# 32 conditioning blocks of a diffusion trunk, multiplied by VectorE during the first input projection

## What is computed

```
ada = silu(cond) @ w_ada[i] + b_ada[i]          # cond: c_ctx and c; 6 x 1024 outputs per layer, 2 layers
sh_m, sc_m, gt_m, sh_f, sc_f, gt_f = split(ada, 6)
h = x * (1 + sc_m) + sh_m
m = ssd_mixer(h) if i == 0 else gdn_mixer(h)    # h @ w_in -> conv -> scan -> norm -> @ w_out
x = layer_norm(ALPHA * x + gt_m * m)
x = layer_norm(ALPHA * x + gt_f * conv_glu_ffn(x * (1 + sc_f) + sh_f))
```

## Time and profile before

| | us |
|---|---|
| median of 3 runs | 1602.67 (1597.7 to 1603.6) |
| profiled execution, whole | 1600.62 |
| its span, first to last instruction | 1598.7 |
| TensorE busy | 1528.4 (96%) |
| VectorE / ScalarE / GpSimd busy | 872.5 / 799.5 / 905.3 |
| input projection, blocks 4 to 48 | about 45.6 to 238.2 |
| scan | about 238.2 to 401.1 |
| DMA queue q1 | 205.96 MB |

### The profile page before, as it was taken

One profiled execution on the slowest core, in us unless ns is written; L12 is line 12 of the kernel. 1 busy time (PEld: TensorE's weight loads), 2 busy tenths in 40 slices (PEclk: granted clock), 3 DMA queues, 4 the chain that ended last, 5 costly groups with the idle time before them and its releaser, 6 DMA issues.

```text
span 1598.7 us, 30956 instructions
## 1 busy us (share of the span) xinstructions
PE 1528.4 (96%) x11737; PEld 1452.6 (91%) x11737; DVE 872.5 (55%) x1814; ACT 799.5 (50%) x1461; POOL 905.3 (57%) x516
## 2 busy tenths in 40 slices
PE   8999999999999999999899999999889999999996
PEld 6999997887989999999899989778778989999996
DVE  3443105776447777613663449598873357777323
ACT  3655436776336544424766563656554345444332
POOL 2555556676563555657146556787763725555552
PEclk9999999999999999999999999999979999999998
DMA  9443437887351443434125323102123423444431
GB/s 376 122 124 114 131 121 269 307 297 279 122 151 56 129 130 120 147 123 152 53 80 173 96 92 104 41 28 54 41 81 119 148 77 106 131 120 139 140 114 40
DMA packets 58018, 209.65 MB, mean 131 GB/s; under 512 B 6320, under 2 KB 6448, under 8 KB 57648
## 3 DMA queue, kind: packets, MB, share of 16 engines
q1 hardware_dynamic: 56752, 205.96, 39.4%
q10 hardware_dynamic: 1152, 2.10, 0.4%
HBM read 200.63 MB, written 7.41 MB: 130 GB/s over the span
## 4 chain that ended last, share of the span: by engine, by line
PE 70%; issue 10%; DVE 9%; POOL 6%; ACT 4%; DMA 2%; POOLq 0%; SPq 0%; DVEq 0%; ACTq 0%
PE ps L900 6%; PE ps L902 6%; PE ps L901 6%; PE ps L808 6%; PE ps L810 6%; PE ps L809 6%; POOL wlo L332 4%; PE ps L1144 3%; PE ps L2884 3%; PE ps L1145 3%; PE ps L1146 3%; PE ps L2885 3%; PE ps L2886 3%; PE ps L402 2%; DVE ps L2457 2%
## 5 line engine op out<-in xcount | busy, mean ns | idle before, releaser
L332 POOL TENSOR_TENSOR wlo<-raw,whi 128x1024 fp32r<-128x1024 f32 (+1 forms) x191 | 484.3, 2536 | 416.0 <-ACT whi L320 415.7
L320 ACT ACTIVATE whi<-raw 128x1024 fp32r<-128x1024 f32 (+1 forms) x237 | 261.4, 1103 | 501.0 <-PE ps L810 186.9
L900 PE MATMUL ps<-hhi,whi 128*128 128x384 f32 x656 | 219.8, 335 | 2.5 <-POOL wlo L332 2.0
L974 DVE SCALAR_TENSOR_TENSOR evac<-ps,vec,evac 128x189 f32<-128x189 f32 (+3 forms) x440 | 166.5, 412 | 99.4 <-ACT evac L915 69.7
L902 PE MATMUL ps<-hhi,wlo 128*128 128x384 f32 x656 | 219.2, 334 | 0.0
L901 PE MATMUL ps<-hlo,whi 128*128 128x384 f32 x656 | 219.1, 334 | 0.0
L2649 POOL TENSOR_TENSOR wlo<-raw,whi 128x1024 fp32r<-128x1024 f32 x46 | 111.2, 2417 | 124.9 <-ACT whi L320 124.9
L2884 PE MATMUL ps<-hhi,whi 128*128 128x384 f32 x368 | 126.3, 343 | 1.7 <-POOL wlo L2649 1.7
L900 PEld LDWEIGHTS ps<-hhi,whi 128*128 128x128 f32 x656 | 123.1, 188 | 4.4 <-issue 3.2
L868 DVE SCALAR_TENSOR_TENSOR xr<-ps,ada,xr 128x128 f32<-128x128 f32 x64 | 23.8, 413 | 183.3 <-PE ps L810 183.2
L2886 PE MATMUL ps<-hhi,wlo 128*128 128x384 f32 x368 | 123.4, 335 | 0.0
(11 more groups left out here) (375 smaller groups left out, 3574.2 us busy)
## 6 DMA issues: line engine op xcount, KB each, us to landing
raw<-w_in_in SPq DMA_DIRECT2D x98, 512.0 KB, 3.6
raw<-w_up_in SPq DMA_DIRECT2D x88, 512.0 KB, 3.5
raw<-w_ada_in SPq DMA_DIRECT2D x80, 512.0 KB, 4.4
raw<-w_down_in SPq DMA_DIRECT2D x32, 704.0 KB, 4.0
raw<-w_out_in SPq DMA_DIRECT2D x32, 512.0 KB, 3.6
first_ada<-w_ada_in SPq DMA_DIRECT2D x16, 512.0 KB, 10.1
qe<-e_keep SPq DMA_DIRECT2D x8, 512.0 KB, 6.7
s<-s_ssd_in SPq DMA_DIRECT2D x8, 256.0 KB, 4.0
```

Source lines behind the costliest of these rows:

```text
L320: act.activation(whi[:, z.mod(SPL), 0:p.kt * P], raw[:, b.mod(RAW), 0:p.kt * P], ACT.Copy).then_inc(hi_ready, 1)
L332: pool.tensor_tensor(wlo[:, z.mod(SPL), 0:p.kt * P], raw[:, b.mod(RAW), 0:p.kt * P], whi[:, z.mod(SPL), 0:p.kt * P].bitcast(F32), ALU.subt ...
L900: pe.matmul(out, a, hhi[:, k, :], start=(k == 0), stop=False)
```

## The change

32 of the 80 later conditioning tiles (eight units of four) are no longer multiplied by TensorE in the scan. Their weights are loaded four blocks at a time (2 MB, two buffers) during the input projection. For each of the two rows of cond, VectorE multiplies the raw weights by silu(cond) as a per-partition scalar and sums over the eight tiles of the model width: 16 instructions of 128x512 per unit, accumulated in PSUM banks 6 and 7, the last of each row writing to SBUF. TensorE then sums the partitions with eight small matmuls per unit (`mid_fold`), after blocks 20, 23, 28, 33, 37, 40, 43 and 46; ScalarE copies the rows one step later, TensorE turns them into columns another step later, VectorE adds the bias. VectorE's products are spread over steps 9 to 32, two or three per step behind the taps; the remaining 59 follow without steps. SyncE issues the first two unit loads ahead of the load of block 8, after a wait for the first four blocks, and the others ahead of the loads of blocks 20, 26, 31, 36, 40 and 43, each after a wait for the products that free its buffer. `ADA_G` becomes 8, 6, 6, 6, 6, 6, 5, 5; the slots in `ssd_pe` are unchanged. The dt chain is moved three steps earlier and its sums to banks 5 and 4.

```diff
+MID = 8
+MID_B = 4
+MID_OPS = 2 * DT
+ADA_M = MID * MID_B
+ADA_2 = 2 * ADA_T - ADA_1 - ADA_M
...
+        MID_AT = (20, 23, 28, 33, 37, 40, 43, 46)
+        MID_LOAD = {20: 2, 26: 3, 31: 4, 36: 5, 40: 6, 43: 7}
+        MID_BIAS = {MID_AT[b] + 2: b for b in range(3)}
+        MID_STEP = {s: 2 if s < 12 else 3 for s in range(9, CONV_T + 1)}
+        MID_BANK, SUM_BANK = 4, 6
+
+        def mid_load(sp, b):
+            if b < 2:
+                sp.wait_ge(blk_done, SPL + FIRST)
+            else:
+                sp.wait_ge(ada_acc, MID_OPS * (b - 1))
+            j = ADA_1 + MID_B * b
+            sp.dma_start(mid_raw[:, b % 2, :, :], io["w_ada"][j:j + MID_B].rearrange("b p n -> p b n")).then_inc(first_in[b % 2], 16)
...
+        def mid_product(dve, m):
+
+            b, t, c = m // MID_OPS, m % MID_OPS // 2, m % 2
+            w = mid_raw[:, b % 2, :, t * P:(t + 1) * P]
+            run = ps[:, SUM_BANK + c, :].rearrange("p (b n) -> p b n", b=MID_B)
+            one = scond[:, t, ZW + c:ZW + c + 1]
+            if t == 0 and c == 0:
+                dve.wait_ge(first_in[b % 2], 64 + 16 * (b // 2 + 1))
+            if m > 1:
+                dve.wait_ge(ada_acc, m - 1)
+            if t == 0:
+                i = dve.tensor_scalar(run, w, one, None, ALU.mult)
+            elif t < DT - 1:
+                i = dve.scalar_tensor_tensor(run, w, one, run, ALU.mult, ALU.add)
+            else:
+                if b and c == 0:
+                    dve.wait_ge(ada_used, ADA_1 + b)
+                i = dve.scalar_tensor_tensor(mid_sum[:, c, :, :], w, one, run, ALU.mult, ALU.add)
+            i.then_inc(ada_acc, 1)
...
+        def mid_fold(pe, b):
+
+            pe.wait_ge(ada_acc, MID_OPS * (b + 1))
+            pe.wait_ge(ada_ready, 1 + DT + b)
+            pe.wait_ge(dt_dec, 1)
+            for n in range(2 * MID_B):
+                q = 32 * (n % 4)
+                mm = pe.matmul(ps[q:q + 32, MID_BANK, 0:P], mid_pick[:, 31 - n:63 - n], mid_sum[:, n % 2, n // 2, :],
+                               tile_position=(0, q), start=(n < 4), stop=(n >= 4))
+            mm.then_inc(ada_used, 1)
+
+        def mid_columns(pe, b):
+            pe.wait_ge(ada_row, DT + b + 1)
+            ada_columns(pe, MID_B, MID_BANK)
...
+                for _ in range(MID_STEP[s] if s in MID_STEP else 0):
+                    mid_product(dve, m)
+                    m += 1
+                if s in MID_BIAS:
+                    mid_bias(dve, MID_BIAS[s])
+            for m in range(m, MID * MID_OPS):
+                if m > 5 * MID_OPS and m % MID_OPS == DT:
+                    mid_bias(dve, m // MID_OPS - 2)
+                mid_product(dve, m)
+            for b in range(MID - 2, MID):
+                mid_bias(dve, b)
...
                 block(s, t % 4)
-                if s == 17:
+                if s == 14:
                     rate_rows()
-                if s == 19:
+                if s == 16:
                     rate_sums()
+                if s in MID_AT:
+                    mid_fold(pe, MID_AT.index(s))
+                if s - 2 in MID_AT:
+                    mid_columns(pe, MID_AT.index(s - 2))
...
-        ADA_G = (0, 14, 24, 34, 44, 53, 62, 71, ADA_2)
+        ADA_G = (0, 8, 14, 20, 26, 32, 38, 43, ADA_2)
...
-            steps(sp, FIRST + RAW, N_IN, lambda j: load_block(sp, sin, j))
+            mid_load(sp, 0)
+            mid_load(sp, 1)
+            for s in range(FIRST + RAW, N_IN):
+                if s in MID_LOAD:
+                    mid_load(sp, MID_LOAD[s])
+                load_block(sp, sin, Idx(s))
```

More of the change, by code:

```diff
@@ L219, in trunk @@
             if name == "ada_first":
-                own_n[kind] += n
+                own_n[kind] += n + MID
                 continue
@@ L270, in trunk @@
         ln_std, ln_stat = sem("ln_std"), sem("ln_stat")
-        x_kept, tri_ready = (sem(x) for x in ("x_kept", "tri_ready"))
+        x_kept, ada_acc = (sem(x) for x in ("x_kept", "ada_acc"))
         def raw_free(sp, at):
@@ new lines, in mid_bias @@
+        def mid_bias(dve, b):
+            dve.wait_ge(ada_tr, DT + b + 1)
+            ada_bias(dve, MID_BANK, ADA_1 + MID_B * b, MID_B).then_inc(ada_ready, 1)
+        def mid_fold(pe, b):
[7 more added lines that the diff above has]
+            mm.then_inc(ada_used, 1)
@@ L597, in h_ready, with mid_rows @@
+        def mid_columns(pe, b):
+            pe.wait_ge(ada_row, DT + b + 1)
+            ada_columns(pe, MID_B, MID_BANK)
+        def mid_rows(act, b):
+            act.wait_ge(ada_used, ADA_1 + b + 1)
+            act.wait_ge(ada_tr, DT + b)
+            ada_rows(act, MID_BANK, MID_B)
         def h_ready(pe, m, k):
@@ L1044, in sums_exp @@
                 act.wait_ge(dt_cum, 1)
-                for c in range(NCH):
-                    i = act.activation(dec_s[:, c, :], ps[:, 6 + c // 2, (c % 2) * NB[0]:(c % 2 + 1) * NB[0]], ACT.Exp)
+                n = NB[0] - 2 * SSD_H
+                for c in range(2):
+                    act.activation(dec_s[:, c, :], ps[:, 5, c * NB[0]:(c + 1) * NB[0]], ACT.Exp)
+                act.activation(dec_s[:, 2, 0:n], ps[:, 5, 2 * NB[0]:2 * NB[0] + n], ACT.Exp)
+                i = act.activation(dec_s[:, 2, n:NB[0]], ps[:, 4, 2 * NB[0]:3 * NB[0] - n], ACT.Exp)
                 i.then_inc(dt_dec, 1)
@@ L1064, in sin_act @@
                     act.wait_ge(consts_in, 48)
-                    act.activation(negtri[:], tri32[:], ACT.Copy).then_inc(tri_ready, 1)
-                if s == 19:
+                    act.activation(negtri[:], tri32[:], ACT.Copy)
+                if s == 16:
                     act.activation(tri_r[:, :, :], masks[:, 3:5, :], ACT.Copy)
@@ L1162, in rate_sums @@
                     a = tok_s[:, 1, c, :]
-                    o = ps[:, 6 + c // 2, (c % 2) * NB[0]:(c % 2 + 1) * NB[0]]
+                    o = ps[:, 5, c * NB[0]:min((c + 1) * NB[0], 512)]
+                    last = o[:, 4 * h:6 * h] if c < 2 else ps[:, 4, 2 * NB[0]:2 * NB[0] + 2 * h]
                     for k, (m, lo, hi) in enumerate((("le", 0, h), ("ge", h, 2 * h), ("gt", 0, h), ("lt", h, 2 * h))):
                         pe.matmul(o[:, k * h:(k + 1) * h], mask(m), a[:, lo:hi], start=True, stop=True)
-                    mm = pe.matmul(o[:, 4 * h:6 * h], ones, a[:, 0:2 * h], start=True, stop=True)
+                    mm = pe.matmul(last, ones, a[:, 0:2 * h], start=True, stop=True)
                 mm.then_inc(dt_cum, 1)
```

65 lines of the change are left out of this document (38 added, 27 removed).

## The result

The changed kernel takes 1605.4 us (median of 20 runs, 1600.2 to 1609.0), the kernel before 1601.9 us (20 runs beside it, 1596.8 to 1604.6): ratio 1.0023, 95% interval 1.0014 to 1.0033. It is slower by some 3.5 us, less than half a per cent. The profiled execution has a span of 1603.9 us; that of before had 1598.7. TensorE's busy time fell by 9 us (1528.4 before) and VectorE's rose by 82 (872.5 before), and the time did not follow either.

The account below looks back on a forecast made before the run. TensorE was taken to bind the projection, while a ScalarE and VectorE chain paces half of each scan group. Projection +9.2 us, scan -6.5, sum +2.7, gave 1603.3 to 1605.4; forecast 1604 us, range 1597 to 1613.

Parts of the forecast that it names:

- Folds and columns: Input projection: eight folds add 6.2 us to TensorE's time and their columns 1.5 us.
- Block 8's load: Projection: two 2.1 MB loads ahead of it in SyncE's queue make block 8 stall 1.5 us, bounds 0 and 3.
- Products 0.75 us, nothing lost: Projection: VectorE's 128 products take 0.75 us each, its step 3.8 us stays under TensorE's 4.16, costing nothing.
- Later loads, nothing up to 3: Projection: loads ahead of blocks 20 to 43 wait for products, tightest at 36; nothing, up to 3 us in all.
- Groups 1 to 6: Scan: period 18.76 us, gaining 0.3 us in each of groups 1 to 3, 0.2 in 4 to 6; 1.6 together.
- Group 0: Scan's first group: six blocks go from three places, 1.0 + 0.6 = 1.6 us gained, bounds 0.5 and 3.0.
- The last group: Scan's end: TensorE binds; output projection starts at about 397.8 instead of 401.15, 3.3 us gained, bounds 1.5 and 3.6.
- Sum +2.7: Whole kernel: projection loses 9.2 us, scan gains 6.5, so +2.7 us; by the bounds -6 to +12.
- The first rival: Scan bound by TensorE: all 32 blocks and the waits for weights come back, 1591 to 1593 us; chance 0.10.
- The second: VectorE becomes the projection's bound in steps 12 to 32, from 0.88 us a product; 1617 us; chance 0.10.
- The third: Projection loads come late again and again, stalling 1 to 2 us each time; +7, 1611 us; chance 0.07.
- The fourth, the clock: Scan: new waits of 0.6 us lower TensorE's clock once in each of seven groups; +10, 1614 us; chance 0.05.

Follow-up runs that it names:

- the fastest kernel here: Changed kernel with moved pairs, moved square_sums, late first loads and second fold at block 24: ratio 0.9918 against the kernel before, median 1590.2 us.

## Why the prediction came out right, step by step

1. *Folds and columns, 6.2 + 1.5 = 7.7 us.* Right: 7.6. A fold costs 0.78 as in the earlier trace rows, and a block behind columns starts 0.14 late and loses 0.09 more.
2. *Block 8's load, 1.5 us.* Right: 1.48, and gone when the loads stand behind it.
3. *Products 0.75 us, nothing lost.* The duration is exact (0.747; the earlier trace rows had the form), and back to back a product costs only 0.66 to 0.67 us, so the step is 3.5 us and not 3.8. But the nothing does not hold: the second fold waited 1.02 us. The step that failed is that only the products were counted, against steps of 4.16 us. What was not priced is the bias of a fold's columns: it stands in VectorE's queue behind the three products of its step, and the next fold, which writes the same bank, waits for it:

```profile
126.62 1.40 DVE L643 SCALAR_TENSOR_TENSOR mid_sum<-mid_raw,scond,ps 128x512 f32<-128x512 f32 x2
...
135.71 2.06 DVE L639 SCALAR_TENSOR_TENSOR ps<-mid_raw,scond,ps 128x512 f32<-128x512 f32 x3
137.69 0.16 DVE L423 TENSOR_TENSOR ada<-ps,vec 128x8 f32<-128x8 f32 x1
```

The second fold's own sums are written by 128.02, the bias is done at 137.85, and the fold starts at 137.94. In the code `mid_fold` waits for both (ada_acc, ada_ready). With one more product before the bias the wait was 1.68 us, with the fold one block later it was gone.

4. *Later loads, nothing up to 3.* 0.30 at block 36, the one called the tightest. With items 1 to 3 that makes 10.4 us; the projection lost 10.9 where 9.2 stood, inside 5.6 to 15, and 0.5 stay without a cause.
5. *Groups 1 to 6, 1.6 us.* Right: from states(1) to states(7) 112.3 us, before 113.9. Period 18.72 where 18.76 stood. With the pairs and the sums moved these six groups took 101.3 us, 11.0 less again, which was no part of this change.
6. *Group 0, 1.6 us.* The trace has 0.9, because TensorE's clock was 0.50 from 262 to 265 us and states(0) took 2.95 us instead of 1.89 (in before it had fallen at 242 already). In the kernel with the blocks left out, whose clock fell where that of before did, it is 1.9. All runs with eight blocks in group 0 fit this: from the scan's start to states(1) they take 28.2 to 28.5 us where the clock did not fall, 28.9 to 29.0 where it fell as in before, and 29.9 to 30.8 where it fell as late as here.
7. *The last group, 3.3 us.* 2.9 in the changed kernel, where a conditioning block still waited 0.73 us for its weights at 398.59 (the late loads didn't all go); 3.4 with the blocks left out. The output projection waits for wlo, as said.
8. *Sum +2.7.* Measured +3.5 by the medians, 5.2 by two single spans. By the traces of the two stages it is 10.9 - 5.5 = 5.4: the projection was priced 1.7 too low and the scan's gain 1.0 too high, so the closeness of 2.7 to 3.5 owes something to luck. The parts are what bears the prediction out. That the sum of the shown median and 2.7 is the measured 1605.4 to the tenth is chance, since that median of three was 0.8 above the one of twenty. The two profiled executions do not differ in their mean clock (0.974 before, 0.975 after).

The first rival (TensorE bound in the scan) is refuted by the kernel with the blocks left out. The second (VectorE) exists: four products a step, as if one took 0.89 us, cost nothing, five, as if one took 1.1, cost 18 us, which is more than its 13 and came in another way, by two waits for small instructions behind the products and by the clock after them. The third gave 0.3 us. The fourth, the clock, did not come where it was placed: after the new waits of 0.6 to 0.7 us the clock stayed at 1.00 in every group, and the earlier trace rows was the right row for that. It fell in group 0, as item 6 tells.

## What to carry to other kernels

A full engine need not be the bound: before moving work off it, take the work away from one period and see what the period does, and read which half of the period another engine paces; work must be taken from the other half. After each gain the next chain is only a microsecond behind (here ScalarE's seg_lo, then GpSimd's additions for a later stage), so the same 32 blocks cost 3.5 us in one order and, with a few instructions moved, saved 13 in another. Count work in an in-order queue by what it stands behind, not by the engine's average share, and count the small instructions too: here a bias of 0.16 us held a fold for 1.02. And where an instruction waits for several semaphores, look up in the code what they are before believing the one that the profile names.

## What the runs showed of the hardware

The place where TensorE's clock falls is not a property of the order alone. Between 0 and 500 us the profiled executions with every fold twice and with moved square_sums had no window with a clock below full speed (the one row for all 500 us of the latter is the first below), the changed kernel's had three stretches, at 262, 419 and 487 us:

```profile
0.00:500.00 500.00, 474.80 (x4046) 432.33 (x4047) 317.63 (x653) 268.07 (x552) 284.80 (x185) 1.00 0.55 194
```
```profile
420.00:422.00 2.00, 2.00 (x7) 2.00 (x8) 1.76 (x4) 0.08 (x1) 2.00 (x1) 0.50 0.54 160
```

By the windows they last 3 to 7 us, and at half clock they cost 1.7 to 3 us each, an estimate that takes half of TensorE's busy time in them. That is as much as most terms of the sum. The same kernel differs too: over the 20 executions of the changed one the mean granted clock was 0.974 in four, which took 1605.8 to 1609.0 us, and 0.981 in three, which took 1600.2 to 1601.7. Effects of this size should be read from the same stage of both traces, and the span of a single execution (1594.9 for the fastest kernel here, 1590.7 for one that is 0.3% slower by its median) does not rank two kernels. The Trainium skill (TensorE: Matmul & The Clock Gate, What's actually happening) says of the slow matmuls at a kernel's start that their number differs from run to run because the gate's own count does not start with the kernel. The runs here agree that the stretches move from one execution to the next, in the middle of a kernel; why they do, no run shows.

A fold of eight 32-column matmuls between full ones costs 0.78 us, of which 0.44 is their number and 0.34 is paid once. And 128x512 products with one operand in PSUM lasted 0.75 us, 0.67 from start to start, beside GpSimd's subtractions throughout; a quarter more of them cost nothing that the medians tell, half more was too much. VectorE's subtractions of 128x384 with both operands in SBUF took 1.79 us on average in the kernel before. The Trainium skill (GPSIMD Engine Reference, Specifications), which has VectorE contend with GpSimd only with two SBUF inputs or in a two-port mode, agrees with this.
